# Value-row loads of a PEER layer moved from SyncE's DMA queue to ScalarE's

## The chip, the cores and the metric

The kernel runs on one core of a Trainium2 chip. A core has TensorE (PE in the profile), VectorE (DVE), ScalarE (ACT), GpSimd (POOL) and SyncE (SP), each with an instruction stream of its own, and 16 DMA engines that all of them share. A transfer is issued by an instruction of SP, ACT or POOL and lands later; semaphores tell who may go on. The metric is the device time of one execution in microseconds (us), of which a run reports the median.

## The reference, cut to what matters

One layer of a hybrid decoder is computed for 512 prompt tokens and 32 sample tokens: a mixer (dilated attention beside a state-space scan), a layer norm, a PEER layer and a second layer norm. Only the PEER layer bears on the change. It has 16384 experts (128 x 128), each a row of `u_tab` and a row of `v_tab` of 1024 numbers, and each token has 8 x 16 of them chosen:

```python
def run_block(args):
    t, g, e = args
    act = jax.nn.gelu(jnp.einsum('nd,nhkd->nhk', t, u_tab[e]), approximate=False)
    return jnp.einsum('nhk,nhkd->nd', g * act, v_tab[e])
```

## The kernel before, in words

For the first three tiles of tokens (`DEN` = 384 tokens) the kernel does not gather: it multiplies all tokens with all 16384 experts, in 128 blocks of 128 experts, and lays a gate matrix over the activations that is zero where an expert wasn't chosen. A first pass (`pe_up`) makes the activations and stores them in DRAM (`act`), with the gates (`gate`). The second pass, the values, is where the change lies: for each block of experts `a` from 0 to 127 it computes out[tokens, 1024] += (gate x activation)[tokens, 128] x V[128, 1024]. For the other 160 tokens the chosen rows of both tables are gathered by GpSimd (`pool_gather`, L1865) into a ring of 8 buffers (`gring`), and VectorE works them off one at a time (L2036, L2041), some between any two blocks.

Numbers are float32, and a product is made of three matmuls on a rounded part and a remainder (L188 to L190). So each block needs these steps:

- a load of the block's value rows, 128 x 1024 numbers or 512 KB, into `vraw[:, k]`. There are four such buffers, k = a mod 4, so the load of block a + 4 may start when VectorE has read block a (semaphore `v_lo`). This is L2104, in `sp_rows`, on SP.
- per group of four blocks (`GRP`): the activations (L2109, 768 KB, in `sp_gelus`) and the gates (L2113, 768 KB in pieces of 512 bytes, in `sp_gates`), two buffers each, also on SP. They may start once VectorE has made the last product of the group before the last (`weighted`).
- VectorE: the product gate x activation (L2236), which at the first block of a group waits for both loads; then the remainder of the value rows (L2240, ends with `v_lo`), a gathered row, the remainder of the product (L2246), and on some blocks a second gathered row.
- ScalarE: the rounded part of the value rows (L2148, waits for the load by `vraw_in`) and of the product (L2152, waits for L2236 by `weighted`).
- TensorE: 18 matmuls of 512 columns. Its inputs have eight buffers each.

SP's order is written out in `sp_values`: for each group the activations, the gates, and then four value loads, each behind its own wait. ScalarE's order is in `act_values`. The last group's VectorE work is mixed with the second layer norm (`final_norm`).

Of the kernel before, what the change touches and what calls it, by code (L numbers as in the profile page):

```python
# [41 lines left out]
GRP = 4  # L42
# [106 lines left out]
def layer(nc, t):  # L149

    ctx = ExitStack()
    with ctx:
        def sem(name):
            return ctx.enter_context(nc.semaphore(name))
# [5 lines left out]
        def overlay(at, *dims, kind=F32):  # L160

            n = len(overlays)
            with nc.sbuf_tensor(f"under{n}", [P, int(at * KW)], F32):
                with nc.sbuf_tensor(f"overlay{n}", [P, int(np.prod(dims))], kind) as tensor:
                    overlays.append((tensor, dims))
            return shaped(tensor[:, :], dims)
# [1197 lines left out]
        def act_root(act, n, i):  # L1364
            act.wait_ge(ln_step.sem, lnm["var", n])
            act.activation(mv[0:rows(i), n % 2, 1:2], mv[0:rows(i), n % 2, 1:2], ACT.Sqrt).then_inc(ln_root, 1)
# [503 lines left out]
        def sp_up(sp):  # L1870
            for s in range(4):
                sp.sem_inc(a_stored[s], 16)
            for s in range(2):
                sp.sem_inc(slab_stored[s], 16)

            def fetch(a, s, free):
                sp.wait_ge(*free)
                sp.dma_start(uraw[s], t["peer_u"][bass.ds(a, 1)].rearrange("a p c n -> p (a c) n")).then_inc(u_in[s], 16)

            def keep(a, s, g):  # L1880

                sp.wait_ge(gelu_done, a + 5)
                sp.dma_start(t["act"][bass.ds(g, 1), :, s].rearrange("g p n -> p (g n)"), aring[:, s]).then_inc(a_stored[s], 16)

            for s in range(4):
                fetch(s, s, (u_lo, s + (QF - 3)))

            def beside(x):
                for s in range(4):
                    fetch(x * 4 + (s + 4), s, (u_lo, x * 4 + (s + QF + 1)))  # L1890
                    keep(x * 4 + (s - KEEP_LAG), (s + 1) % 4, x + (s - KEEP_LAG) // 4)

            for s in range(4):
                fetch(s + 4, s, (u_lo, s + QF + 1))
            keep(0, 0, 0)
            with sp.Fori(1, EARLY // 4) as x:
                beside(x)

            def keep_slab(n):
                sp.wait_ge(g_kept, n * GS + (GS + 4))  # L1900
                sp.dma_start(t["gate"][n], slab[n % 2]).then_inc(slab_stored[n % 2], 16)

            def next_row(a):
                if a + 4 < PK:
                    fetch(a + 4, a % 4, (u_lo, QF + a + 1) if a < EARLY + LEAD else (u_lo2, a - (EARLY + LEAD) + 1))
                if a >= EARLY:
                    keep(a - KEEP_LAG, (a - KEEP_LAG) % 4, (a - KEEP_LAG) // 4)

            for n in range(SLABS):
                if n:  # L1910
                    keep_slab(n - 1)
                for k in range(UPS):
                    next_row(EARLY + n * UPS + k)
            sp.wait_ge(slab_stored[0], 16 * (1 + SLABS // 2))
            for k in range(GRP):
                sp_rows(sp, 0, 0, k)
            sp.wait_ge(hot_ready, DEN // 4)
            for s in range(4):
                sp.wait_ge(a_stored[s], 32)
            sp_gelus(sp, 0, 0)  # L1920
            keep_slab(SLABS - 1)
            for a in range(TAIL, PK):
                next_row(a)
                if a == TAIL + 3:
                    sp.wait_ge(slab_stored[1], 16 * (1 + SLABS // 2))
                    sp_gates(sp, 0, 0)
            for a in range(PK - KEEP_LAG, PK):
                keep(a, a % 4, a // 4)
# [159 lines left out]
        vraw, vs = overlay(10, 4, D), (overlay(152, 8, D, kind=F32R), overlay(75, 8, D, kind=F32R))  # L2088
# [3 lines left out]
        vraw_in = [sem(f"vraw_in{s}") for s in range(4)]  # L2092
        v_hi, v_lo, ga_hi, ga_lo, weighted, vp_done = (sem(n) for n in ("v_hi", "v_lo", "ga_hi", "ga_lo", "weighted", "vp_done"))
# [3 lines left out]
        ROWS_END, FINAL_AT, BY_TILE = PK - 8, (PK - 7, PK - 5), 4  # L2097
        LATE_ROWS = 2 * UROWS - EARLY_ROWS - DONE

        def sp_rows(sp, x, par, k):  # L2100

            a = x * 8 + (par * GRP + k)
            sp.wait_ge(v_lo, a + 1)
            sp.dma_start(vraw[:, k], t["peer_v"][bass.ds(a, 1)].rearrange("a p n -> p (a n)")).then_inc(vraw_in[k], 16)  # L2104

        def sp_gelus(sp, x, par):
            g = x * 2 + par
            sp.wait_ge(weighted, g * GRP + 4)
            sp.dma_start(agrp[par], t["act"][bass.ds(g, 1)].rearrange("g p k n -> p (g k) n")).then_inc(a_in[par], 16)  # L2109

        def sp_gates(sp, x, par):
            g = x * 2 + par
            sp.dma_start(ggrp[par].rearrange("p (s a n) -> p s (a n)", a=GRP, n=SLAB),  # L2113
                         t["gate"].rearrange("s p a n -> p s (a n)")[:, :, bass.ds(g * (GRP * SLAB), GRP * SLAB)])\
                .then_inc(gate_in[par], 16)

        def sp_values(sp):
            for s in range(2):
                sp.wait_ge(slab_stored[s], 16 * (1 + SLABS // 2))
            for s in range(4):  # L2120
                sp.wait_ge(a_stored[s], 16 * (1 + 2))
            sp.wait_ge(u_done, PK)

            def group(x, par):
                sp_gelus(sp, x, par)
                sp_gates(sp, x, par)
                for k in range(GRP):
                    sp_rows(sp, x, par, k)

            group(0, 1)  # L2130
            for s in range(4):
                sp.wait_ge(a_stored[s], 16 * (GROUPS + 1))
            with sp.Fori(1, PAIRS - 1) as x:
                for par in range(2):
                    group(x, par)
            group(PAIRS - 1, 0)
            sp_norm2(sp)
            group(PAIRS - 1, 1)
            sp.wait_ge(copied, 16 * 48)

        def act_values(act):

            def pair(x, last=False):
                for j in range(8):
                    par, k = j // GRP, j % GRP
                    act.wait_ge(vp_done, x * 8 + (j + 1))
                    act.wait_ge(vraw_in[k], x * 32 + (16 * par + 16))
                    act.copy(vs[0][:, j], vraw[:, k]).then_inc(v_hi, 1)  # L2148
                    if last and j in (2, 4):
                        act_root(act, TILES + j // 2 - 1, LAST[j // 2 - 1])  # L2150
                    act.wait_ge(weighted, x * 8 + (j + 9))
                    act.copy(ga[0][:, j], prod[j % 2]).then_inc(ga_hi, 1)  # L2152

            act.wait_ge(row_done, SLOTS)
            act.activation(w3, w3, ACT.Gelu).then_inc(w_gelu, 1)
            with act.Fori(0, 2) as x:
                pair(x)
            act.wait_ge(row_done, UROWS)
            act.activation(wS, wS, ACT.Gelu).then_inc(w_gelu, 1)
            with act.Fori(2, PAIRS - 1) as x:  # L2160
                pair(x)
            pair(PAIRS - 1, last=True)
# [101 lines left out]
        def sp_norm2(sp):  # L2264
            sp.wait_ge(row_done, EARLY_ROWS + max(last_row(4), last_row(5)))
            sp.dma_start(lng2, t["ln2_g"]).then_inc(ln2_in, 16)
            sp.dma_start(lnb2, t["ln2_b"]).then_inc(ln2_in, 16)
# [60 lines left out]
        @block.scalar  # L2328
        def _(act):
            act.sem_inc(silu_done, 1)  # L2330
            act_consts(act)
            act_project(act)
            act_attend(act)
            act_ssd_run(act)
            act_out(act)
            act_query(act)
            act_up(act)
            act_values(act)
            act_final(act)
# [19 lines left out]
        @block.sync  # L2359
        def _(sp):  # L2360
            sp_project(sp)
            sp_states(sp)
            sp_attend(sp)
            sp_ssd(sp)
            sp_out(sp)
            sp_dump5(sp)
            sp_query(sp)
            sp_up(sp)
            sp_values(sp)
            sp_final(sp)  # L2370
            sp.wait_ge(stored, stores[0])
# [68 lines left out]
```

## Time and profile before

| what | value |
|---|---|
| median of 3 runs | 2135.26 us (2133.72 to 2141.08) |
| the profiled execution's own time | 2126.72 us |
| its span, first to last instruction | 2124.8 us |
| TensorE busy in the span | 2039.0 us (96%), granted clock 0.983 |
| VectorE, ScalarE, GpSimd busy | 1493.5, 741.0, 781.4 us |
| DMA moved | 682.98 MB, mean 321 GB/s |
| value pass, first to last L2148 | 1564.5 to 2100.3 us |

Busy time is the time in which an engine computes; waiting and the issuing of transfers are not counted. "Landing" of a transfer is the time from the start of its issue to its semaphore. A wait is idle time of an engine, put down to what ended it. The share of the DMA engines can come out somewhat above 1, because packets on one engine overlap.

### The profile page before, as it was taken

Reading aid. Unit: us, or ns where it says so; the run is one execution under the profiler, and the core shown is the slowest. Engines: PE = TensorE matmul, PEld = TensorE weight load, DVE = VectorE, ACT = ScalarE, POOL = GpSimd, SP = SyncE. Lnnn points to the kernel's source line nnn. Section 1 sums busy time; section 2 is a strip of 40 time slices with the busy share of each in tenths; the row PEclk is TensorE's granted clock in tenths of the full one; section 3 lists DMA queues with packets and bytes.
Section 4 is the critical chain, followed back from the end, with each engine's and each line's share of the span. In section 5 each row is a group of like instructions: output and inputs, shape, how many; then the busy total and the mean of one; then the engine's idle time right before and its main releaser. Section 6 shows DMA issues by size and latency. Waiting matters only on the chain.

```text
span 2124.8 us, 33666 instructions
## 1 busy us (share of the span) xinstructions
PE 2039.0 (96%) x12186; PEld 1703.1 (80%) x12186; DVE 1493.5 (70%) x3108; ACT 741.0 (35%) x1111; POOL 781.4 (37%) x485
## 2 busy tenths in 40 slices
PE   7999999998879999999999999999999999999998
PEld 7999985555553347999999999999988777877876
DVE  1386125664662334679888699999789888888988
ACT  3232113444430002224333355555433333333332
POOL 4343310000210003347889731221365555555530
PEclk9999998999978999999999999999999999999999
DMA  9999887884968669847999878887999999999993
GB/s 330 353 320 344 307 328 283 346 353 171 334 225 329 236 219 364 351 134 271 351 361 355 310 283 304 301 306 280 386 397 391 392 392 392 392 384 387 386 370 141
DMA packets 202346, 682.98 MB, mean 321 GB/s; under 512 B 18304, under 2 KB 84224, under 8 KB 194176
## 3 DMA queue, kind: packets, MB, share of 16 engines
q1 hardware_dynamic: 150832, 439.29, 56.7%
q0 software_dynamic: 46080, 167.79, 20.6%
q10 hardware_dynamic: 5328, 74.52, 9.9%
q8 instruction: 62, 1.02, 0.2%
q14 instruction: 44, 0.36, 0.0%
HBM read 618.78 MB, written 196.32 MB: 384 GB/s over the span
## 4 chain that ended last, share of the span: by engine, by line
PE 68%; DMA 19%; DVE 8%; issue 2%; ACT 2%; SPq 0%; POOL 0%; DVEq 0%; ACTq 0%; POOLq 0%
DMA overlay<-peer_v 16%; PE bank L188 15%; PE bank L189 15%; PE bank L190 15%; PE bank L1426 5%; PE bank L2028 4%; DVE overlay L2240 2%; DVE arena L2041 2%; PE bank L644 2%; PE bank L628 2%; ACT overlay L2148 1%; PE bank L667 1%; PE bank L694 1%; DMA arena<-cache_v 1%; PE bank L998 1%
## 5 line engine op out<-in xcount | busy, mean ns | idle before, releaser
L188 PE MATMUL bank<-overlay 128*128 128x384 f32 (+4 forms) x2832 | 959.5, 339 | 35.6 <-DVE overlay L2246 17.4
L189 PE MATMUL bank<-overlay 128*128 128x384 f32 (+4 forms) x2832 | 944.7, 334 | 0.0
L190 PE MATMUL bank<-overlay 128*128 128x384 f32 (+4 forms) x2832 | 943.8, 333 | 0.0
L188 PEld LDWEIGHTS bank<-overlay 128*128 128x128 f32 (+1 forms) x2832 | 532.8, 188 | 80.5 <-issue 45.4
L190 PEld LDWEIGHTS bank<-overlay 128*128 128x128 f32 (+1 forms) x2832 | 532.2, 188 | 31.3
L189 PEld LDWEIGHTS bank<-overlay 128*128 128x128 f32 (+1 forms) x2832 | 532.9, 188 | 30.1
L1865 POOL DMA_INDIRECT arena<-peer_v,arena x160 | 261.1, 1632 | 224.9 <-DVE arena L2041 207.8
L1586 POOL TENSOR_TENSOR overlay<-overlay 128x1024 fp32r<-128x1024 f32 x86 | 206.7, 2405 | 295.9 <-ACT overlay L1579 292.1
L2041 DVE SCALAR_TENSOR_TENSOR arena<-arena 128x1024 f32<-128x1024 f32 x160 | 205.4, 1284 | 0.1
L1579 ACT CAST overlay<-overlay 128x1024 fp32r<-128x1024 f32 x144 | 150.1, 1044 | 143.0 <-DMA overlay<-peer_u 84.6
L1865 POOL DMA_INDIRECT arena<-peer_rows,arena x80 | 106.4, 1330 | 244.7 <-DVE arena L2036 223.8
L2240 DVE TENSOR_TENSOR overlay<-overlay 128x1024 fp32r<-128x1024 f32 x128 | 156.7, 1224 | 44.0 <-ACT overlay L2148 44.0
L2148 ACT CAST overlay<-overlay 128x1024 fp32r<-128x1024 f32 x128 | 134.4, 1050 | 140.5 <-DMA overlay<-peer_v 140.4
L358 POOL TENSOR_TENSOR overlay<-overlay 128x1024 fp32r<-128x1024 f32 x44 | 106.5, 2429 | 172.2 <-ACT overlay L320 172.2
L1938 ACT ACTIVATE arena<-bank 128x384 f32<-128x384 f32 x128 | 63.9, 499 | 209.9 <-PE bank L190 206.3
L2152 ACT CAST overlay<-overlay 128x384 fp32r<-128x384 f32 x128 | 65.7, 513 | 196.9 <-DVE overlay L2236 196.7
L1426 PE MATMUL bank<-arena 128*128 128x512 f32 x256 | 118.9, 616 | 0.0
L1977 ACT COPY arena<-bank 128x512 f32<-128x512 f32 x96 | 103.7, 1131 | 35.6 <-PE bank L2028 35.6
L1726 DVE SCALAR_TENSOR_TENSOR arena<-arena,bank 128x1024 f32<-128x1024 f32 x80 | 96.2, 1214 | 23.8 <-DMA arena<-peer_rows,arena 23.7
L2072 DVE TENSOR_SCALAR arena<-arena 128x128 f32<-128x128 f32 x384 | 107.1, 357 | 0.0
L1426 PEld LDWEIGHTS bank<-arena 128*128 128x128 f32 x256 | 48.5, 196 | 65.5 <-issue 64.0
L2028 PE MATMUL bank<-arena 128*128 128x128 f32 x768 | 101.0, 274 | 0.0
(235 smaller groups left out, 2166.2 us busy)
## 6 DMA issues: line engine op xcount, KB each, us to landing
overlay<-peer_u SPq DMA_DIRECT2D x128, 512.0 KB, 7.4
overlay<-peer_v SPq DMA_DIRECT2D x128, 512.0 KB, 11.8
o_ks<-cache_k ACTq DMA_DIRECT2D x11, 4088.0 KB, 18.2
o_vsall<-cache_vall SPq DMA_DIRECT2D x21, 2044.0 KB, 24.9
arena<-cache_kT SPq DMA_DIRECT2D x32, 896.0 KB, 11.7
arena<-cache_v SPq DMA_DIRECT2D x56, 512.0 KB, 6.6
arena<-w_out SPq DMA_DIRECT2D x48, 512.0 KB, 5.6
act<-arena SPq DMA_DIRECT2D x128, 192.0 KB, 8.3
```

The source lines that it names most:

```text
L188: pe.matmul(out, lhs[0], rhs[0], start=start, stop=False)
L189: pe.matmul(out, lhs[0], rhs[1], start=False, stop=False)
L190: return pe.matmul(out, lhs[1], rhs[0], start=False, stop=stop)
L1426: mm = pe.matmul(bank[:, 2 * (i % 2) + half, :], mixT[:, c, i * P:(i + 1) * P], w[:, half * 512:(half + 1) * 512], start=(c == 0), stop=(c ...
L1579: act.copy(us[0][:, s], uraw[s]).then_inc(u_hi, 1)
L1586: pool.tensor_tensor(us[1][:, s], uraw[s], us[0][:, s].bitcast(F32), ALU.subtract).then_inc(u_lo, 1)
L1865: pool.indirect_dma_start(gring[g % RING], None, table, bass.IndirectOffsetOnAxis(ap=at, axis=0)).then_inc(row_in[g % RING], 16)
L2028: mm = pe.matmul(bank[:, 4 + w % 4, j * P:(j + 1) * P], hot_b[:, w % 2, j], hot_a[:, w % 2, j], start=True, stop=True)
L2041: dve.scalar_tensor_tensor(acc, gring[r], w[:, bass.ds(j, 1)], acc, ALU.mult, ALU.add).then_inc(row_done, 1)
L2072: mm = dve.tensor_scalar(hot_b[:, w % 2, j], const("iota"), at(1), at(2), ALU.is_equal, ALU.mult)
L2148: act.copy(vs[0][:, j], vraw[:, k]).then_inc(v_hi, 1)
L2240: dve.tensor_tensor(vs[1][:, j], vraw[:, k], vs[0][:, j].bitcast(F32), ALU.subtract).then_inc(v_lo, 1)
```

## The change

The issue of value loads is taken from SP, but for the first four, and put behind the cast of the product on ScalarE: after block a ScalarE waits for `v_lo` of block a and issues the load of block a + 4. The last four blocks issue nothing. SP keeps activations and gates. The waits that guard the buffers are the same ones.

```diff
-        def sp_rows(sp, x, par, k):
-
-            a = x * 8 + (par * GRP + k)
-            sp.wait_ge(v_lo, a + 1)
-            sp.dma_start(vraw[:, k], t["peer_v"][bass.ds(a, 1)].rearrange("a p n -> p (a n)")).then_inc(vraw_in[k], 16)
+        def value_rows(eng, x, j):
+
+            a = x * 8 + j
+            eng.wait_ge(v_lo, a + 1)
+            eng.dma_start(vraw[:, j % GRP], t["peer_v"][bass.ds(a, 1)].rearrange("a p n -> p (a n)")).then_inc(vraw_in[j % GRP], 16)
...
                 sp_gelus(sp, x, par)
                 sp_gates(sp, x, par)
-                for k in range(GRP):
-                    sp_rows(sp, x, par, k)
...
                     act.wait_ge(weighted, x * 8 + (j + 9))
                     act.copy(ga[0][:, j], prod[j % 2]).then_inc(ga_hi, 1)
+                    if not last or j + GRP < 8:
+                        value_rows(act, x, j + GRP)
```

On ScalarE, at the first block of a loop over pairs of groups, there stood before (CAST of 128x1024 is the value rows' rounded part, CAST of 128x384 the product's):

```order
668 L2147 ISA [waits vp_done]
669 L2148 CAST overlay<-overlay 128x1024 [waits vraw_in0]
670 L2151 REGISTER_ALU
671 L2152 CAST overlay<-overlay 128x384 [waits weighted]
672 L2146 REGISTER_ALU
673 L2148 CAST overlay<-overlay 128x1024 [waits vraw_in1,vp_done]
```

And now, at the same place:

```order
669 L2146 CAST overlay<-overlay 128x1024 [waits vraw_in0]
670 L2149 REGISTER_ALU
671 L2150 CAST overlay<-overlay 128x384 [waits weighted]
672 L2103 REGISTER_ALU
673 L2104 ISA [waits v_lo]
674 L2104 DMA overlay<-peer_v 128x1024
675 L2144 REGISTER_ALU
676 L2146 CAST overlay<-overlay 128x1024 [waits vraw_in1,vp_done]
```

A wait for `v_lo` and an issue now stand between the casts of one block and the next.

On SP, in the loop over pairs of groups, there stood before, for the first group of a pair (REGISTER_ALU rows compute addresses):

```order
305 L2109 DMA arena<-act 128x1536
306 L2113 ISA
307 L2113 DMA arena<-gate 128x12x128
308 L2103 ISA
309 L2104 ISA [waits v_lo]
310 L2104 DMA overlay<-peer_v 128x1024
311 L2103 REGISTER_ALU
312 L2104 ISA [waits v_lo]
313 L2104 DMA overlay<-peer_v 128x1024
```

And now:

```order
304 L2109 DMA arena<-act 128x1536
305 L2113 ISA
306 L2113 DMA arena<-gate 128x12x128
307 L2108 ISA
308 L2109 ISA [waits weighted]
309 L2109 DMA arena<-act 128x1536
```

Behind a group's gates the next thing on SP is now the next group's activations. TensorE's, VectorE's and GpSimd's orders are unchanged.

## Rows read from the trace of the kernel before

**Rows 1.** Busy time of each engine in two stretches of the value pass.

```profile
core 0: us, PE busy (x) PEld busy (x) DVE busy (x) ACT busy (x) POOL busy (x), PEclk, DMA share, GB/s
1600.00:2043.00 443.00, 432.03 (x1883) 351.65 (x1883) 392.19 (x458) 156.55 (x210) 243.28 (x146) 1.00 1.04 390
2043.00:2104.00 61.00, 58.80 (x250) 45.68 (x249) 57.92 (x75) 24.76 (x35) 6.78 (x4) 1.00 0.74 262
```

**Rows 2.** A group of instructions by line, 1600 to 2050 us.

```profile
L188 PE MATMUL bank<-overlay 128*128 128x512 f32 x636 | 249.7, 393 | 12.3 <-DVE overlay L2246 11.8
```

**Rows 3.** Waits, 1600 to 2050 us: total us, times, longest.

```profile
ACT overlay L2148 <- DMA overlay<-peer_v: 132.4, 59, 6.2
DVE overlay L2240 <- ACT overlay L2148: 40.0, 21, 2.9
DVE overlay L2236 <- issue: 11.3, 11, 2.2
```

**Rows 4.** The chain that ended last, in time: start, us.

```profile
1719.90 15.65 DMA overlay<-peer_v
...
1735.58 1.06 ACT overlay L2148
...
1736.66 1.24 DVE overlay L2240
...
1738.05 13.01 DMA overlay<-peer_v
```

**Rows 5.** Stretches of 4 us (columns as in rows 1).

```profile
1720.00:1724.00 4.00, 4.00 (x19) 3.34 (x18) 4.00 (x5) 2.00 (x3) 3.16 (x2) 1.00 1.03 409
1724.00:1728.00 4.00, 4.00 (x19) 3.30 (x19) 4.00 (x6) 1.47 (x2) 2.88 (x2) 1.00 1.09 353
```

**Rows 6.** DMA queues and issues, 1600 to 2050 us.

```profile
DMA packets 81979, 175.23 MB, mean 389 GB/s; under 512 B 4917, under 2 KB 46091, under 8 KB 81970
...
q1 hardware_dynamic: 60694, 97.68, 60.3%
q0 software_dynamic: 21276, 77.46, 44.1%
...
overlay<-peer_v SPq DMA_DIRECT2D x106, 512.0 KB, 11.9
...
arena<-gate SPq DMA_DIRECT2D x26, 768.0 KB, 16.9
arena<-peer_v,arena POOLq DMA_INDIRECT x148, 9.1
```

**Rows 7.** DMA queues in two single microseconds, 1738 and then 1744 us.

```profile
q1 hardware_dynamic: 49, 0.21, 51.5%
q0 software_dynamic: 49, 0.20, 50.3%
...
q0 software_dynamic: 74, 0.30, 82.7%
q1 hardware_dynamic: 97, 0.08, 25.3%
```

**Rows 8.** SP's instructions in time, 1731 to 1743.9 us: start, us.

```profile
1731.52 0.33 SPq L2109 DMA_DIRECT2D arena<-act  x1
1732.04 0.38 SPq L2113 DMA_DIRECT2D arena<-gate  x1
1738.05 5.68 SPq L2104 DMA_DIRECT2D overlay<-peer_v  x1
```

**Rows 9.** Line 2104, 1600 to 2050 us: duration ns min/median/max.

```profile
L2104 SPq DMA_DIRECT2D overlay<-peer_v x106: 332/333/8306, 1601.8 to 2049.6; - x106
```

**Rows 10.** Line 950, stores that ScalarE issues: duration ns min/median/max.

```profile
L950 ACTq DMA_DIRECT2D o_hs<-arena x8: 338/339/371, 657.2 to 720.4; - x8
```

**Rows 11.** VectorE in time, L2240 of two blocks.

```profile
2074.32 1.23 DVE L2240 TENSOR_TENSOR overlay<-overlay 128x1024 fp32r<-128x1024 f32 x1
...
2076.39 1.23 DVE L2240 TENSOR_TENSOR overlay<-overlay 128x1024 fp32r<-128x1024 f32 x1
```

More of the change, by code:

```diff
@@ L1915, in sp_up @@
             for k in range(GRP):
-                sp_rows(sp, 0, 0, k)
+                value_rows(sp, 0, k)
             sp.wait_ge(hot_ready, DEN // 4)
```

## The prediction, made before the changed kernel ran

> **What bounds the kernel now.** I read the profile from the outside in: first which engine is full in the value pass, then what the pass waits for, then whether that thing has room to give.
>
> In the stretch from 1600 to 2043 us TensorE is busy for 432 of 443 us at the full granted clock, VectorE for 392, and the DMA engines show a share of 1.04 at 390 GB/s [rows 1]. Three things are nearly full at once. TensorE did 636 / 6 = 106 blocks between 1600 and 2050 us (six products of this line to a block), so a block takes 450 / 106 = 4.25 us and a group of four 17.0 us; TensorE was idle for 12.3 us of the 450, nearly all behind VectorE's last step on a block [rows 2]. VectorE in turn was idle for 40.0 us behind ScalarE's cast of value rows and for 11.3 us at L2236 for nothing that the view names [rows 3]; L2236 is where a group's activations and gates are waited for, so I read those eleven as gates. That makes (450 - 51.3) / 106 = 3.76 us of VectorE's own work per block. ScalarE waited 132.4 us for value loads, 59 times [rows 3]. The chain of waits shows the ring: a load of 15.65 us, the cast, VectorE's remainder, the next load of 13.01 us [rows 4]. Four buffers and about 17 us from one use of a buffer to the next are just the 4.25 us per block.
>
> So the value load is what comes last. Why does it take so long? A transfer of 512 KB at 389 GB/s alone would be 1.35 us; the median is 11.9 us and that of the gates 16.9 us [rows 6]. They queue. In both 4 us stretches shown the DMA share is above 1, whether VectorE just waited or not, at 409 GB/s without many gate pieces and at 353 with them [rows 5]. Per block 175.23 MB / 106 = 1.65 MB move [rows 6], and 1.65 MB / 389 GB/s = 4.25 us: the DMA engines' total work explains the pace by itself. For TensorE to run without its idle time (4.13 us per block) they would have to move 400 GB/s.
>
> A second thing stands in SP's stream. After the activations and gates of a group are issued (0.33 and 0.38 us), a value load's issue holds SP for 5.68 us, from 1738.05 to 1743.73 [rows 8]. The median issue of the line is 333 ns, the longest 8306 ns [rows 9]. SP doesn't compute, so this costs only the loads behind it.
>
> **The change, part by part.**
>
> *Issue instructions.* 124 loads move from SP to ScalarE. ScalarE's issues of a similar store take 339 ns [rows 10], so 124 x 0.34 = 42 us of sequencer time. ScalarE is busy for 157 of 443 us [rows 1]; the room is there. What counts is the order: after block a it now waits for VectorE's L2240 (1.24 us), issues (0.34) and only then casts the next rows (1.06) [rows 4, 10]: 2.64 us, against 3.76 us in which VectorE comes round. Hidden, cost 0. If this cover were gone, each 0.1 us per block would be 12 us. It is gone in one place: in the last groups VectorE does a block without gathered rows in 2076.39 - 74.32 = 2.07 us [rows 11]. Of the last eight blocks only the first four issue, and the layer norm covers one step of these, so two steps are longer by 0.6 to 0.9 us: +1 to +2 us. I take +1.5.
>
> *The value load is no longer behind the gates in one queue.* When both queues are full of large packets they share evenly (49 packets each, 51.5% and 50.3%); when SP's queue has gates at its head it makes 97 packets and 0.08 MB to the gathers' 74 and 0.30 MB [rows 7]. So turns go by packet, and 512-byte pieces lose. In a queue of its own a value load has every third turn at worst and should land sooner than 11.9 us. The wait of 132.4 us at the cast should shrink to a fraction. But the bytes are the same, the share is already full, so what the value rows gain the gathers and gates lose. In the steady part: 0. Bound above: all of TensorE's idle time, -12.3 us, which needs the 400 GB/s. Bound below: 0 from this part alone.
>
> *A loan, taken once.* The gathered rows are early now: 148 in 450 us is one per 3.04 us, eight buffers last 24.3 us, and they land after 9.1 us [rows 6]. Some 15 us x 1 row / 3.04 us = 5 rows, 2.6 MB or 6.6 us of DMA work, stand ready ahead of need. If value rows take turns from them, this stock can be spent once: 0 to -6.6 us. But then value rows are stocked instead, and from 2043 us on the DMA share is 0.74 [rows 1], so stock is worth little at the end. I take -1.5, nearer to 0.
>
> *SP.* Its activations and gates no longer stand behind four value waits; they are issued about 1 to 2 us sooner and are not behind loads that were issued earlier. They compete with them, though. Between a gate load's 16.9 us and the group's 17.0 us there is next to nothing. Cost 0, see the third rival.
>
> Sum against the profiled execution: 2126.7 + 1.5 - 1.5 = 2126.7 us. The median of the runs shown is 8.5 us above that execution; so the forecast for the changed kernel's median is 2135 us, no change.
>
> The even sharing and the full share are the rows' own; the Trainium skill, page "DMA: Bandwidth & Descriptors", section "Issuing engines are not separate DMA queues", states the rule that speaks against this change: transfers issued by different engines run on the same 16 DMA engines and interleave, and issuing from several saves only issue time. By that rule the steady part is 0; by the wait rows alone (132.4 us of waiting for value loads) one would have summed up to the 12.3 us of TensorE's idle time.
>
> **The rivals.**
>
> *Forecast, chance 0.45: the DMA total bounds.* The wait at the cast shrinks, another (gathers at L2041, or L2236) grows, the pace stays 4.25 us. 2130 to 2141 us.
>
> *Slower, 0.31: the hold moves to ScalarE.* What held SP for 5.68 us behind the gates may hold any engine that issues at that time. ScalarE, unlike SP, has casts to do; VectorE has 3.76 - 1.24 = 2.5 us of other work after L2240, then it waits. A hold of 5.68 us stalls it for 3.2 us, and a group takes 4 x 3.76 + 3.2 = 18.2 us in place of 17.0: +1.2 us in 30 groups, +36 us. It decides from a hold of 2.5 + (17.0 - 15.0) = 4.5 us on; below that the DMA total still rules. At 8.3 us in every group it would be +3.8 x 30 = +114 us, which I don't believe, since a stalled pass leaves fewer packets ahead of the gates. Against it: the median issue is short, in this execution no issue of ScalarE's fell into a hold of SP's, and two engines may be held apart. I price it at +20, between 0 and +36: 2155 us.
> On this rival the Trainium skill, same page, section "Queues, rings and completion order", says that SP and ACT each own a row of rings but have no descriptor generator of their own. By that, an issue of ScalarE's could stand behind SP's gates; no row here shows it.
>
> *Slower, 0.04: gates starve.* With two queues of 4096-byte packets against them, the gates' 1536 small packets get one turn in three and land after more than the 17 us plus 2.5 that they have. The DMA engines stay full meanwhile, so the price is small: half a microsecond per group, +15 us, 2150 us. L2236 would show it.
>
> *Faster, 0.20: the order was the loss.* TensorE's idle time goes, because DMA turns now go to what is needed next and the small pieces mix with large ones. -12.3 x 536 / 450 = -14.6 us at most for the whole pass (1564.5 to 2100.3), about -10 us likely: 2125 us. For it: the chain runs through loads. Against it: the share of 1.04.
>
> That the change does nothing of what it says can be left out: the order on both engines shows it.
>
> **How the numbers follow.** About 0.3% (6.4 us) is what a measurement of this kernel can tell from no change. The forecast's 0.45 lies within it, as do some 0.05 of the holding rival (holds under 4.5 us) and 0.03 of the faster one; 0.04 of the forecast's chance is noise to the sides. Faster 0.21, same 0.48, slower 0.31. The range leaves out 1 in 10 below and above: from the faster case's bound less a little, 2121 us, to the holding rival at 2158 us. The likeliest case's own range is 2129 to 2141 us.
>
> **What would show each step.** In the profile of the changed kernel: a third queue with 124 loads; L2104's landing well under 11.9 us, L2148's wait for loads below 60 us; DMA 385 to 395 GB/s at a share above 1 between 1600 and 2040 us; 106 blocks in 450 us. The hold would show as issues on ScalarE of over 1 us, some 30 of them, and as a longer wait of L2240 for L2146. If the DMA share falls below 1 in the steady part, the step "the DMA total bounds" is wrong; if it stays and GB/s rises to 400, the faster case is right. The prediction fails most likely by the hold.

## The result, and the profile after

| | before | after |
|---|---|---|
| median, us (4 runs each) | 2138.17 (2133.72 to 2147.1) | 2186.42 (2182.49 to 2193.44) |
| the profiled execution's own time | 2126.72 | 2182.49 |
| value pass, first to last cast of value rows | 535.8 | 582.6 |
| from the last cast to the end | 24.5 | 24.5 |

The changed kernel is slower by 2.2%: ratio 1.0217, 95% interval 1.0178 to 1.0256. That lies outside the range of 2121 to 2158 us. The medians lie 48.3 us apart, the two profiled executions 55.8 us: the value pass accounts for 46.8 of these, and the other 9.0 stand before it (see "Open").

Busy time by engine of the changed kernel, the same two stretches as [rows 1]:

```profile
core 0: us, PE busy (x) PEld busy (x) DVE busy (x) ACT busy (x) POOL busy (x), PEclk, DMA share, GB/s
1600.00:2043.00 443.00, 406.24 (x1704) 331.19 (x1705) 361.51 (x428) 150.59 (x193) 227.58 (x134) 0.95 0.97 353
2043.00:2104.00 61.00, 57.72 (x248) 47.28 (x247) 49.70 (x59) 20.91 (x27) 34.48 (x19) 0.97 1.00 365
```

TensorE and VectorE are both less busy, and the DMA share is under 1: 353 GB/s where 390 flowed. No engine took over as the bound. Waits, 1600 to 2050 us (total, times, longest), which answer to [rows 3]:

```profile
ACT overlay L2146 <- DVE overlay L2240: 99.7, 80, 1.5
DVE overlay L2236 <- issue: 81.4, 12, 8.9
PE bank L188 <- DVE overlay L2246: 40.8, 11, 6.8
...
ACT overlay L2146 <- DMA overlay<-peer_v: 1.2, 1, 1.2
```

ScalarE hardly waits for value rows any more (1.2 us, were 132.4). VectorE waits at L2236, the product with the gates, for 81.4 us in twelve waits (were 11.3 in eleven); the view names no transfer for it, but the activations, the other thing waited for there, land after 9.2 us, and the chain of one such wait, below, names the gates. DMA queues and issues in the same stretch, beside [rows 6]:

```profile
DMA packets 73779, 158.90 MB, mean 353 GB/s; under 512 B 4449, under 2 KB 41125, under 8 KB 73770
...
q0 software_dynamic: 19348, 70.48, 41.3%
q10 hardware_dynamic: 13903, 50.66, 29.9%
q1 hardware_dynamic: 40519, 37.67, 26.1%
...
overlay<-peer_v ACTq DMA_DIRECT2D x98, 512.0 KB, 7.6
...
arena<-gate SPq DMA_DIRECT2D x24, 768.0 KB, 21.3
arena<-peer_v,arena POOLq DMA_INDIRECT x137, 10.4
```

The new queue q10 carries the value rows, q1 activations and gates. A value load lands after 7.6 us in place of 11.9, a gate load after 21.3 in place of 16.9. 98 blocks were done, not 106: 450 / 98 = 4.59 us each.

**Where the time sits.** Take VectorE's waits out and divide by the blocks. Before this gave 3.76 us; after, (450 - 81.4) / 98 = 3.76 us as well. VectorE's own work did not change. Waits per block rose from (40.0 + 11.3) / 106 = 0.48 to 81.4 / 98 = 0.83 us, and 0.35 us by 128 blocks are some 44 us, of the 46.8 measured.

**One stall.** The timeline of SP's issues between 1700 and 1724 us, then VectorE's first product after it (start, duration, what, in brackets the idle time before it):

```profile
1701.20 0.33 SPq L2109 DMA_DIRECT2D arena<-act  x1
1701.72 0.38 SPq L2113 DMA_DIRECT2D arena<-gate  x1
```

```profile
1713.02 0.56 DVE L2236 TENSOR_TENSOR overlay<-arena 128x384 f32<-128x384 f32 x1 [7.99 <-issue]
```

The chain of waits puts this on a gate load that was issued one group earlier, at 1687.45:

```profile
1687.45 17.58 DMA arena<-gate
1705.03 7.99 issue
```

17.58 + 7.99 = 25.6 us from issue to use. The landing of that load, and of the next one, issued at 1701.72, in the view of DMA issues of their single microseconds:

```profile
arena<-gate SPq DMA_DIRECT2D x1, 768.0 KB, 25.5
...
arena<-gate SPq DMA_DIRECT2D x1, 768.0 KB, 16.2
```

The two after these, issued at 1725.27 and about 1740.7, took 22.4 and 15.6 us. About every second group is late; the other one's gates were issued only 14 us behind and are there when needed. Over the 450 us the landings spread from 13.8 to 26.4 us, before from 14.3 to 20.6. What the DMA engines did meanwhile, in stretches of 2 us (columns as above):

```profile
1706.00:1708.00 2.00, 2.00 (x11) 1.65 (x10) 0.00 (x0) 0.00 (x0) 0.24 (x1) 1.00 1.03 404
...
1714.00:1716.00 2.00, 0.00 (x0) 0.00 (x0) 2.00 (x3) 0.81 (x2) 0.00 (x0) 1.00 0.84 226
1718.00:1720.00 2.00, 2.00 (x6) 1.52 (x6) 2.00 (x3) 1.05 (x1) 0.55 (x1) 0.50 0.89 279
1722.00:1724.00 2.00, 2.00 (x11) 1.62 (x10) 2.00 (x3) 0.95 (x1) 1.35 (x2) 1.00 0.76 252
```

From 1706 to 1708 VectorE stands idle while the engines run full, at 404 GB/s: mostly with value rows, gathers and the next group's activations, which nobody needs yet. In the microsecond from 1708 us value rows and gathers have a share of 0.84, out of 1.03 in all. Then those buffers are full, and at 1714 and 1722 the share is 0.84 and 0.76. TensorE stands still from 1714 to 1716. The queues in the single microseconds from 1703, 1711 and 1714 us show both halves:

```profile
q10 hardware_dynamic: 49, 0.19, 48.6%
q0 software_dynamic: 49, 0.18, 45.0%
q1 hardware_dynamic: 41, 0.02, 7.5%
...
q0 software_dynamic: 81, 0.29, 75.1%
q1 hardware_dynamic: 79, 0.12, 32.3%
...
q1 hardware_dynamic: 475, 0.26, 94.6%
q0 software_dynamic: 3, 0.01, 3.2%
```

At 1703 three queues get 49, 49 and 41 packets: turns by packet. The gates make 0.02 MB with their turns, the others 0.18 and 0.19. At 1711, when value rows have nothing left to load, the two queues that are left get 81 and 79. Single microseconds scatter (at 1744 us of the kernel before, q1 had 97 to 74); over those between 1600 and 2050 us in which all three queues had more than 20 packets and nearly all of q1's were gate pieces (119 of them), the medians are 50, 60 (the gates) and 47. At 1714 the small pieces have the engines to themselves and make 0.26 MB at a share near 1, which is less than the 0.39 of the mix. The Trainium skill, page "DMA: Bandwidth & Descriptors", section "Queues, rings and completion order", says that an engine goes round the queues it has work for and changes after a packet, which it puts at some 9 to 17 descriptors. The trace agrees on the going round, not on that size: the counts are near equal piece by piece, so a turn here looks like one piece, of 512 or of 4096 bytes.

### The profile page after: what moved, and what is told of

Read it like the earlier page. It is cut to its first block, busy times and chain, and to the rows that moved or that the text cites. A ratio compares the mean times of both kernels' runs of the same rounds, so it can differ in the third digit from the quotient of the medians.

```text
span 2180.6 us, 33555 instructions
## 1 busy us (share of the span) xinstructions
PE 2057.9 (94%) x12186; PEld 1717.7 (79%) x12186; DVE 1490.9 (68%) x3108; ACT 749.1 (34%) x1111; POOL 791.0 (36%) x485
## 4 chain that ended last, share of the span: by engine, by line
PE 65%; DMA 15%; DVE 10%; issue 8%; ACT 1%; POOL 1%; SPq 0%; DVEq 0%; ACTq 0%; POOLq 0%
PE bank L188 15%; PE bank L189 14%; PE bank L190 14%; DMA arena<-gate 10%; PE bank L1426 5%; PE bank L2028 4%; DVE arena L2041 3%; DVE overlay L2240 2%; PE bank L644 2%; PE bank L628 2%; DMA overlay<-peer_wq 1%; PE bank L694 1%; PE bank L667 1%; DVE overlay L2246 1%; PE bank L635 1%
## 5 line engine op out<-in xcount | busy, mean ns | idle before, releaser
L188 PE MATMUL bank<-overlay 128*128 128x384 f32 (+4 forms) x2832 | 966.9, 341 | 67.8 <-DVE overlay L2246 49.7
L1865 POOL DMA_INDIRECT arena<-peer_v,arena x160 | 271.9, 1699 | 261.6 <-DVE arena L2041 236.1
L2240 DVE TENSOR_TENSOR overlay<-overlay 128x1024 fp32r<-128x1024 f32 x128 | 156.3, 1221 | 2.3 <-ACT overlay L2146 2.3
L2236 DVE TENSOR_TENSOR overlay<-arena 128x384 f32<-128x384 f32 x128 | 71.0, 555 | 102.9 <-issue 102.8
```

Source lines behind the costliest of these rows:

```text
L188: pe.matmul(out, lhs[0], rhs[0], start=start, stop=False)
L1865: pool.indirect_dma_start(gring[g % RING], None, table, bass.IndirectOffsetOnAxis(ap=at, axis=0)).then_inc(row_in[g % RING], 16)
L2240: dve.tensor_tensor(vs[1][:, j], vraw[:, k], vs[0][:, j].bitcast(F32), ALU.subtract).then_inc(v_lo, 1)
```

## The experiments

Two theories were open. **Turns**: a gate load is 1536 pieces of 512 bytes; with value rows in a queue of their own it stands against two queues of 4096-byte packets, loses the engines' time by turns, and lands late. **Rivals**: the changed order on ScalarE (its wait for `v_lo`) costs, or a third queue costs by itself. Each run had the kernel before beside it on the same chip; its medians there were 2139.25 (first four runs), 2135.74 (next four) and 2141.13 us (last two), and each ratio is to that kernel. Line numbers differ by a few between the kernels; the text says what stands on a line. Stretches of 450 us are 1600 to 2050, and 1620 to 2070 where the value pass begins later.

**Activations and gates to ScalarE, value loads stay on SP.** ScalarE's order is another than in the changed kernel, the separation the same.

```diff
-                sp_gelus(sp, x, par)
-                sp_gates(sp, x, par)
...
+                    if j % GRP == 3 and not last:
...
+                        sp_gelus(act, x + 1, j // GRP)
+                        sp_gates(act, x + 1, j // GRP)
```

> Value loads stay on SP, and ScalarE issues activations and gates instead, so the queues are separate as in the changed kernel but ScalarE never waits for VectorE's remainder of the value rows. Theory (turns): the gates, alone with the activations in a queue, lose turns by packet to two queues of 4096-byte packets whoever issues them; gates land after 20 to 26 us in about every second group, and the median is 2175 to 2195 us. Rival (order on ScalarE): the added wait on ScalarE costs the time; then this kernel is back at 2132 to 2145 us with gates landing in about 17 us.

Measured 2189.12 us, ratio 1.0215 (1.014 to 1.0291): all of the loss, with ScalarE issuing no value load. VectorE's wait at the product, and below it the gates in the view of DMA issues:

```profile
DVE overlay L2245 <- issue: 95.0, 13, 10.7
```

```profile
arena<-gate ACTq DMA_DIRECT2D x24, 768.0 KB, 18.6
```

(450 - 95.0) / 96 blocks = 3.70 us: VectorE's own work again. The gates land after 18.6 us in the median, but about every second load takes 20 to 26, as expected. Which engine issues what doesn't matter, that the two are apart does.

**The issue a block later.** In the changed kernel the issue moves behind the next block's cast, where `v_lo` has long come.

```diff
-                    if not last or j + GRP < 8:
-                        value_rows(act, x, j + GRP)
...
+                    if not last or j + GRP - 1 < 8:
+                        value_rows(act, x, j + GRP - 1)
```

> The changed kernel, but ScalarE issues a value load one block later, behind its next cast, where the wait for VectorE has already been met. Theory (turns): no change from the changed kernel, 2178 to 2195 us, L2236 still waits 80 us or more, and ScalarE's wait for L2240 (99.7 us in 450) is gone. Rival (order on ScalarE): most of the 48 us come back, below 2155 us.

Measured 2193.42 us, ratio 1.0245 (1.017 to 1.032). ScalarE's wait for L2240 (99.7 us in the changed kernel) is gone from the waits, and nothing was gained:

```profile
DVE overlay L2236 <- issue: 90.7, 12, 11.0
```

So the order on ScalarE is out as a cause.

**Gates in large pieces.** The gate array is laid out in DRAM so that a group's gates are 6144 contiguous bytes for each partition. The stores of the first pass get the 512-byte pieces in its stead. Made with the kernel before and with the changed one.

```diff
-                sp.dma_start(t["gate"][n], slab[n % 2]).then_inc(slab_stored[n % 2], 16)
+                sp.dma_start(t["gate"][:, :, n].rearrange("g p m -> p g m"), slab[n % 2].rearrange("p (g a) n -> p g (a n)", a=GRP)).then_inc(slab_stored[n % 2], 16)
...
-    t["gate"] = nc.dram_tensor("gate", (DEN // SLAB, P, PK, SLAB), F32, kind="Internal").ap()
+    t["gate"] = nc.dram_tensor("gate", (PK // GRP, P, DEN // SLAB, GRP * SLAB), F32, kind="Internal").ap()
```

> The kernel before, with the gates laid out in DRAM so that a group's load is one 6144-byte piece per partition; the stores of the gates, in the first pass, are then in pieces of 512 bytes. Theory (turns): gates cost about as much DMA time as activations, so a group needs less than 17.0 us and comes near TensorE's own 16.5 us: the value pass is 8 to 15 us shorter. The first pass gets longer by 0 to 20 us. Median 2120 to 2145 us. Rival (the number of queues): says nothing of this one.

> The changed kernel with the same layout of the gates. Theory (turns): large gate pieces hold their turns, gates land in under 17 us, L2236's wait falls from 81 us to under 15 us, and the kernel is within 8 us of the previous one with large pieces on SP alone. Rivals (order on ScalarE; a third queue costs by itself): it stays 35 to 50 us above that kernel.

With the kernel before 2153.72 us (1.0063, 1.003 to 1.0095), with the changed one 2154.48 us (1.0069, 1.0033 to 1.0105): 2.2% between the two have become 0.04%. The value pass is 517.1 and 516.5 us long, 19 us shorter than in the kernel before, more than the 8 to 15 expected. DMA issues, first with the queues of before, then with those of the change, and last the wait that VectorE has left in the second:

```profile
DMA packets 46676, 184.70 MB, mean 410 GB/s; under 512 B 5181, under 2 KB 5181, under 8 KB 46665
...
overlay<-peer_v SPq DMA_DIRECT2D x111, 512.0 KB, 11.5
...
arena<-gate SPq DMA_DIRECT2D x28, 768.0 KB, 14.9
```

```profile
overlay<-peer_v ACTq DMA_DIRECT2D x112, 512.0 KB, 8.3
...
arena<-gate SPq DMA_DIRECT2D x28, 768.0 KB, 12.5
arena<-peer_v,arena POOLq DMA_INDIRECT x158, 19.8
```

```profile
DVE arena L2041 <- DMA arena<-peer_v,arena: 26.4, 23, 3.4
```

In the second kernel the gates, now in the largest pieces of all, land after 12.5 us; the gathers are last in line, 19.8 us, and VectorE's small wait has moved to them. The time of the first kernel missed its range (2120 to 2145 us): that neither kernel gained in all is the first pass, which I had not looked at and had priced at 0 to 20 us. In the first of the two the value pass begins at 1610.8 us, in the kernel before at 1564.5 and in the seven others with the old stores at 1569.3 to 1579.3. SP issues the small-piece stores and is then held at the next load, as its timeline shows:

```profile
1255.33 0.40 SPq L1901 DMA_DIRECT2D gate<-arena  x1
1255.77 5.24 SPq L1878 DMA_DIRECT2D overlay<-peer_u  x1
```

**Stores of the gates issued by ScalarE.** To give back that hold: `keep_slab` runs in ScalarE's stream at the end of each slab, beside the large pieces.

```diff
-                if n:
-                    keep_slab(n - 1)
...
+                keep_slab(act, n)
```

> The kernel before with the gates in 6144-byte pieces for the load, as in the third kernel, and the gate stores of the first pass (now 512-byte pieces) issued by ScalarE in its own queue, so that SP's loads of key rows are not behind them. Theory: the 46 us that the first pass lost with this layout were loads queued behind the stores on SP; here the value pass still takes 517 us and starts at 1565 to 1590 us: 2108 to 2135 us. Rival: the small stores themselves cost DMA time and turns wherever they are issued; then the value pass starts after 1600 us again, 2145 to 2160 us.

> The same on top of the changed kernel (value loads on ScalarE). Theory (turns): with large pieces it makes no difference which queue the value rows have, within 6 us of the previous kernel.

With the queues of before 2125.5 us, ratio 0.9942 (0.9915 to 0.997); with those of the change 2128.63 us, 0.9961 (0.9934 to 0.9988). The value pass of the first begins at 1580.2 us and takes 516.8, both as expected. Both beat the kernel before, and where value loads are issued makes no difference that these runs tell. TensorE is busy for all of the 450 us in both; the line is of the first:

```profile
sum 450.00, PE 450.00 PEld 372.75 DVE 417.05 ACT 166.07 POOL 250.16; mean PE 450.00 PEld 372.75 DVE 417.05 ACT 166.07 POOL 250.16
```

**Gates behind the value load of a group's last block, in one queue.** In the changed kernel ScalarE issues the gates too, right behind a value load; only activations stay on SP. Later value rows can't overtake these gates.

```diff
-                sp_gates(sp, x, par)
...
+                    if j % GRP == 3 and not last:
+                        sp_gates(act, x + 1, j // GRP)
```

> The changed kernel, but the gates of a group are issued by ScalarE too, right behind the load of block 4g + 3, so gates and value rows stand in one queue in order, and only the activations are apart. Theory (turns): value rows that are behind the gates can no longer run ahead of them; the pace of before comes back, 2130 to 2150 us, gates land in 16 to 18 us, unless ScalarE is held. The rival on record in the prediction (a hold on the issuing engine): ScalarE's issues of value rows behind the gates last 4 to 8 us once a group, and the median is 2150 us or more.

Measured 2164.48 us, ratio 1.0123 (1.0073 to 1.0174). The gates land after 13.9 us in the median, the wait for them nearly goes; but ScalarE is held at its next issue, and its casts come late for VectorE. Waits (L2147 is the cast of value rows, L2243 VectorE's remainder of them, L2239 the product):

```profile
ACT overlay L2147 <- issue: 108.7, 32, 7.9
...
DVE overlay L2243 <- ACT overlay L2147: 65.0, 33, 5.6
...
DVE overlay L2239 <- issue: 11.4, 1, 11.4
```

One such issue in ScalarE's timeline:

```profile
1720.58 6.31 ACTq L2104 DMA_DIRECT2D overlay<-peer_v  x1
```

Somewhat less than half of the loss came back (1.23% is left of 2.17%), outside the 2130 to 2150 us of the turns theory and within the 2150 us or more of the rival. What is left is mainly another thing: the hold that the prediction feared, and which the change itself doesn't have.

**Only the pieces' size, for the gates.** The changed kernel reads six pieces of 1024 bytes for each partition in place of twelve of 512, the same bytes from other places, so the PEER layer of the first three tiles is computed from wrong gates.

```diff
-                         t["gate"].rearrange("s p a n -> p s (a n)")[:, :, bass.ds(g * (GRP * SLAB), GRP * SLAB)])\
+                         t["gate"].rearrange("s p a n -> p s (a n)")[:, 0:6, bass.ds(g * 64, 2 * GRP * SLAB)])\
```

> The changed kernel, but a group's gates are read as six pieces of 1024 bytes per partition from another part of the gate array: same bytes, half the packets, and the outputs of the PEER layer are computed from wrong gates. Theory (turns by packet): 48 packets per engine and group in place of 96 need half the turns; gates land in 12 to 18 us, and nearly all of the 48 us are gone: 2120 to 2145 us. Rival (a third queue, or ScalarE's order): 2175 us or more.

Measured 2135.8 us, ratio 0.9996 (0.9965 to 1.0026): the loss is gone, with queues, order, bytes and stores of the changed kernel. The value pass takes 539.0 us, before 535.8. Packets and issues, then the wait:

```profile
DMA packets 60871, 174.92 MB, mean 389 GB/s; under 512 B 4914, under 2 KB 24882, under 8 KB 60862
...
arena<-gate SPq DMA_DIRECT2D x27, 768.0 KB, 19.4
```

```profile
DVE overlay L2236 <- issue: 49.7, 13, 6.1
```

The time came as expected, the landing did not: 19.4 us in the median and 23.6 at most, not 12 to 18, and VectorE still waits 49.7 us at the product. That is what it waited in all in the kernel before (51.3 us, most of it then for casts), and so the pace is the same. A third queue has no price of its own that these runs show. VectorE's own work is (450 - 49.7) / 107 = 3.74 us for a block. This run lowers the engines' work for gates as well as the gates' handicap in turns, so it doesn't part these two.

**The pieces' size of the value rows.** The other way round: value loads of the changed kernel in 1024-byte pieces. They come from other places of the same rows, so the PEER layer of the first three tiles is computed from wrongly ordered value rows.

```diff
-            eng.dma_start(vraw[:, j % GRP], t["peer_v"][bass.ds(a, 1)].rearrange("a p n -> p (a n)")).then_inc(vraw_in[j % GRP], 16)
+            eng.dma_start(vraw[:, j % GRP].rearrange("p (b m) -> p b m", b=4),
+                          t["peer_v"][bass.ds(a, 1)].rearrange("a (b r) (q m) -> (r q) (a b) m", b=4, q=4)).then_inc(vraw_in[j % GRP], 16)
```

> The changed kernel, but each value load is made of 512 pieces of 1024 bytes in place of 128 of 4096 (the same bytes, read from other places of the same expert's rows, so PEER outputs are computed from wrongly ordered value rows). The opposite dose to the run with gates in 1024-byte pieces: here the rivals of the gates are made smaller. Turns theory: a turn of the value queue now carries 1 KB, so a value load needs four times the turns, lands later than 7.6 us (10 us or more), and the gates land sooner: median under 19 us, none over 23, the swing of 25 and 15 us between neighbouring groups gone, VectorE's wait at the product under 50 us (82 in the changed kernel). The time is then 2150 to 2180 us; not less, because 1024-byte pieces cost more engine time for each byte (46 ns for about 930 bytes against 150 ns for 4096 in the changed kernel's records: up to +0.4 us for a load). Rival (the third queue, or ScalarE's order, costs by itself, whatever the sizes): gates land as in the changed kernel, 21 us in the median with 26 at most, and the time is 2186 us or more.

Measured 2168.75 us, ratio 1.0122 (1.0076 to 1.0168). The time is in the range of the turns theory, and the interval lies below that of the changed kernel (1.0178 to 1.0256), though the engines have more packets to make, 116015 in place of 73779. This parts what the run before left together: smaller rivals help the gates even where the engines' work grows. Value loads land later and VectorE waits less at the product, as expected (DMA issues, then waits: L2147 is the cast of value rows, L2241 VectorE's remainder, L2237 the product):

```profile
overlay<-peer_v ACTq DMA_DIRECT2D x101, 512.0 KB, 14.1
...
arena<-gate SPq DMA_DIRECT2D x25, 768.0 KB, 20.8
```

```profile
ACT overlay L2147 <- DMA overlay<-peer_v: 173.1, 65, 6.3
...
DVE overlay L2237 <- issue: 36.1, 11, 9.8
```

The gates' median landing was a miss: 20.8 us, not under 19. The engines are full all the time now (a share of 1.06 from 1600 to 2043 us), which I take for the reason; no run shows it. But the swing between groups is gone as expected: landings lie between 17.5 and 23.6 us, where the changed kernel had 13.8 to 26.4. 101 blocks were done, not 98, and the engines don't run dry. ScalarE waits for value rows again (173.1 us), and VectorE for its casts (38.4 us), so part of the loss stays: a value pass of 567.5 us, before 535.8 and in the changed kernel 582.6.

**Half of the loads.** In the changed kernel ScalarE issues the loads of odd blocks only; those of even blocks stand behind the gates in SP's queue.

```diff
+                for k in (0, 2):
+                    value_rows(sp, x, par * GRP + k)
...
-                    if not last or j + GRP < 8:
+                    if j % 2 and (not last or j + GRP < 8):
```

> The changed kernel, but only the loads of odd blocks are issued by ScalarE; those of even blocks stand again in SP's queue behind the group's gates. Turns theory: only half of the value rows can overtake the gates, so gates land between 17 and 21 us in the median, VectorE's wait at the product is 20 to 60 us of the 450, and the time lies between the two kernels, 2150 to 2175 us. If overtaking needs only two loads to fill the share of turns, it comes near the changed kernel (2180). Rival (ScalarE's order costs): half the loads behind the cast, half the loss, 2162 us, but with the gates' landing unchanged at 17 us. Rival (a third queue costs by itself): 2186 us.

Measured 2148.23 us, ratio 1.0023 (0.9993 to 1.0053): near the kernel before, 2 us under the expected range. Gate landing and wait (19.0 us, at the lower edge of the expected 20 to 60) lie between the two kernels:

```profile
arena<-gate SPq DMA_DIRECT2D x26, 768.0 KB, 18.4
```

```profile
DVE overlay L2238 <- issue: 19.0, 10, 8.2
```

Half of the value loads on ScalarE cost about a tenth of the loss by the ratios (0.23% of 2.17%, by this run's interval at most a quarter) and a sixth by the value pass (543.8 us, 8.0 more than before, of 46.8): the price isn't in proportion. I read it so: as long as two loads of four wait behind the gates, value rows can't get far ahead.

## Why the prediction was wrong

**The step that failed** is "But the bytes are the same, the share is already full, so what the value rows gain the gathers and gates lose. In the steady part: 0", and its twin in the third rival, "The DMA engines stay full meanwhile, so the price is small". The share was full because SP's one queue kept value rows behind the gates. Apart, the value rows ran ahead until their four buffers were full, the gates got only turns of 512 bytes, and when VectorE stood still nothing else could be started: the share fell to 0.97 in the mean, which the prediction had named as the sign that this step is wrong, and the rate to 353 GB/s. The bytes of a block stayed (158.90 / 98 = 1.62 MB, before 1.65), but the rate at which they move was no constant.

**The right mechanism was on record and mis-sized.** The third rival, that gates starve, had a chance of 0.04 and a price of +15 us. L2236 showed it, as the text said it would. Its size: 46.8 us over 32 groups is 1.5 us for each, not 0.5. The gates' landing of 21 us in the median hides two values, 25 and 16 us; the late one costs some 7 us at L2236 (81.4 / 12) in every second group, less what VectorE no longer waits for casts. I had compared a landing of "more than the 17 us plus 2.5" with the group's mean period and left out that the late one stops those who issue the other loads.

**Right.** The value load lands well under 11.9 us (7.6) and the wait at its cast falls below 60 us (1.2). The issue on ScalarE is 344 ns, and its wait behind L2240 is hidden (the later issue changed nothing). The time from the last cast to the end is 24.5 us in both kernels, so the +1.5 of the last groups is not seen at that place; whether it is within the pass can't be told apart. The -1.5 of the loan isn't seen either.

**Two slips that decided nothing.** The chances of faster, same and slower don't quite follow from the parts named: these give about 0.19, 0.49 and 0.32, not 0.21, 0.48 and 0.31. And "whether VectorE just waited or not" isn't what [rows 5] show: VectorE is busy for all of both stretches.

**The hold on ScalarE** (chance 0.31) didn't come. All of its 124 issues lie between 334 and 375 ns:

```profile
L2104 ACTq DMA_DIRECT2D overlay<-peer_v x124: 334/344/375, 1576.0 to 2143.9; - x124
```

The hold belongs to the engine that issued the small pieces: with the gates in ScalarE's own queue it was up to 6.9 us. **The faster case** (0.20) fell by its condition: the DMA turns did not go to what was needed next. While VectorE waited for gates, at 1708 us, most of the engines' time went to value rows and gathers.

The rule cited in the prediction, that issuing engines aren't separate queues and interleave (the Trainium skill, page "DMA: Bandwidth & Descriptors", section "Issuing engines are not separate DMA queues"), made me sure of 0. The runs agree that nothing is gained by a second issuer; they add that it cost 2.2% here.

**Open.** The value pass of the changed kernel begins 9.0 us later in its profiled execution than that of before (1573.5 and 1564.5 us); the medians differ by 48.3 us and the pass by 46.8. In the six other kernels with the same first pass the value pass begins between 1569.3 and 1579.3 us, also in the one whose value loads all stay on SP (1575.9), and the profiled execution of before was a fast one (2126.72 us, below all four runs in the table). So the 9.0 us look like the spread between executions and not like the change; what makes the spread stays open. Whether the engines lose more by running dry or by having small pieces alone was not separated. With a third buffer for gates late landings should do no harm; that wasn't tried.

## What to carry to other kernels

Before taking loads out of a shared queue, look at what that queue's order held back: a first-in, first-out queue in which small pieces stand ahead of large ones protects the small ones, and DMA engines that take turns by packet don't. Compute the pace as the engine's own work for a block plus its waits (here 3.7 to 3.8 us in every kernel), and ask which transfer is last once the present last one is early; a full DMA share is a result of that, not a constant. Where small pieces lose, make them larger at the source: 1024 bytes in place of 512 took the whole loss away (in a kernel that read other gates than it should), and 6144 made the choice of queue irrelevant and, with the stores on ScalarE, a kernel 0.6% faster than before.

## What the runs showed of the hardware

- Three busy queues got 49, 49 and 41 packets in a microsecond, of 4096, 4096 and 512 bytes, and two got 81 and 79: a queue's rate goes by its pieces' size.
- 512-byte pieces alone filled the engines at 0.26 MB in a microsecond; large and small mixed made 0.39 in the other one shown.
- In the two passes of the PEER layer issues of SP and ScalarE were held for more than 4 us (the 5.24, 6.31 and, before, 5.68 us; 13.0 at most, in the changed kernel with large gate pieces) only where the engine's own earlier transfer was of many small pieces: SP behind gate loads and gate stores, ScalarE behind gate loads once it issued these, and neither across. Shorter holds, up to 3.8 us, were seen on SP in the first pass too, and holds of 4 to 10 us on SP ahead of it (a store of `o_vs` at 255 us, a load of `ln_b` at 621 us), whose cause wasn't looked for.
- After TensorE's idle stretch from 1714 to 1716 us its granted clock was 0.50 from 1718 to 1720, which is 1.2 in place of 2.4 GHz: six matmuls in 2 us, not eleven. So the stall cost TensorE its time twice, standing still and then slow. VectorE's waits account for 44 of the 46.8 us by themselves, so the slow stretch isn't shown to have made the kernel longer.
